# Three edits to a hybrid decoder layer on one core: condition and products moved at the start, output chunks fetched together, PE's feed-forward loop written out

## The reference, cut to what matters

```python
shift1, scale1, gate1, shift2, scale2, gate2 = adaln_terms(c, w_ada, b_ada)
h = rms_norm(x, g_pre_mix) * (1.0 + scale1) + shift1
z = einsum('btd,de->bte', h, w_in)
...
merged = (sigmoid(gm) * einsum('btw,wd->btd', hm, w_proj_m)
          + sigmoid(gd) * einsum('btw,wd->btd', hd, w_proj_d))
y = einsum('btd,de->bte', merged, w_out)
x = x + gate1 * rms_norm(y, g_post_mix)
h2 = rms_norm(x, g_pre_ffn) * (1.0 + scale2) + shift2
u = einsum('btd,df->btf', h2, w_up)           # a half: causal conv of width 3, then GELU
out = einsum('btf,fd->btd', gelu(conv(a)) * b, w_down)
x = x + gate2 * rms_norm(out, g_post_ffn)
```

## Time and profile before

| | us |
|---|---|
| three timed runs | 1811.71, 1811.73, 1812.12 |
| median | 1811.73 |
| the profiled execution, its own time | 1811.7 |
| its span in the profile | 1810.0 |
| PE busy in the span | 1749.2 (97%) |
| VectorE busy | 752.5 (42%) |
| ScalarE busy | 500.9 (28%) |
| GpSimd busy | 156.9 (9%) |

### The profile page before, as it was taken

How to read it: one execution, slowest core, us unless ns; L and a number is a source line. 1 busy time by engine, 2 the same in 40 slices (tenths; PEclk the granted TensorE clock), 3 DMA queues, 4 the chain that set the end, 5 groups by cost and what they waited for, 6 DMA issues and landing times. The chain is left out here.

```text
span 1810.0 us, 27372 instructions
## 1 busy us (share of the span) xinstructions
PE 1749.2 (97%) x11470; PEld 1655.8 (91%) x11470; DVE 752.5 (42%) x1017; ACT 500.9 (28%) x810; POOL 156.9 (9%) x231
## 2 busy tenths in 40 slices
PE   5999999999999999999999999999999999999998
PEld 5899888888888989999978899999999999999997
DVE  5522144544431146564543344424434434344245
ACT  4311134434343334431233331111211211211212
POOL 4010000000010014400023300000000000000001
PEclk8999999999999999999999999999999999999999
DMA  9665342232227577443432211111111021011104
GB/s 324 224 201 180 111 132 78 99 110 87 87 66 250 170 208 184 113 116 125 168 131 85 74 50 47 47 48 47 47 48 47 24 71 47 24 56 48 38 25 172
DMA packets 159707, 190.41 MB, mean 105 GB/s; under 512 B 13694, under 2 KB 138126, under 8 KB 159565
## 3 DMA queue, kind: packets, MB, share of 16 engines
q1 hardware_dynamic: 139368, 170.95, 29.5%
q10 hardware_dynamic: 19208, 17.43, 3.0%
q0 software_dynamic: 1008, 0.23, 0.1%
HBM read 146.70 MB, written 41.87 MB: 104 GB/s over the span
## 5 line engine op out<-in xcount | busy, mean ns | idle before, releaser
L158 PE MATMUL ps<-mg_hi,w_hi 128*128 128x352 f32 x1008 | 218.5, 325 | 6.0 <-issue 2.9
L158 PE MATMUL ps<-mg_hi,w_lo 128*128 128x352 f32 x1008 | 217.3, 323 | 0.0
L158 PE MATMUL ps<-mg_lo,w_hi 128*128 128x352 f32 x1008 | 217.0, 323 | 0.0
L158 PEld LDWEIGHTS ps<-mg_hi,w_hi 128*128 128x128 f32 x1008 | 171.4, 189 | 7.7 <-issue 5.6
L158 PEld LDWEIGHTS ps<-mg_hi,w_lo 128*128 128x128 f32 x1008 | 173.0, 188 | 0.0
L158 PEld LDWEIGHTS ps<-mg_lo,w_hi 128*128 128x128 f32 x1008 | 171.2, 188 | 0.0
L2808 DVE TENSOR_TENSOR f_t<-f_t,ps 128x1056 f32<-128x1056 f32 x80 | 100.3, 1253 | 151.2 <-PE ps L158 151.2
L143 DVE TENSOR_TENSOR w_lo<-w_raw,w_hi 128x2048 fp32r<-128x2048 f32 x61 | 141.3, 2316 | 51.6 <-ACT w_hi L139 51.6
L139 ACT ACTIVATE w_hi<-w_raw 128x2048 fp32r<-128x2048 f32 x61 | 116.7, 1914 | 121.1 <-PE ps L158 120.0
L1221 PE MATMUL ps<-acts_hi,w_hi 128*128 128x352 f32 x384 | 133.5, 348 | 8.1 <-ACT out_z L1074 3.8
L1337 PE MATMUL ps<-acts_hi,w_hi 128*128 128x352 f32 x384 | 128.6, 335 | 4.9 <-PEq L994 1.6
(11 more groups left out here) (412 smaller groups left out, 3066.8 us busy)
## 6 DMA issues: line engine op xcount, KB each, us to landing
w_raw<-in_w_in SPq DMA_DIRECT2D x22, 1024.0 KB, 5.8
w_raw<-in_w_up SPq DMA_DIRECT2D x22, 1024.0 KB, 5.1
w_ada_chunks<-in_w_ada ACTq DMA_DIRECT2D x16, 1024.0 KB, 7.6
w_raw<-in_w_down SPq DMA_DIRECT2D x11, 1024.0 KB, 4.9
z_scratch<-out_z SPq DMA_DIRECT2D x48, 176.0 KB, 1.8
z_scratch<-gate_ev SPq DMA_DIRECT2D x48, 176.0 KB, 3.7
w_ada_chunks<-in_w_ada SPq DMA_DIRECT2D x8, 1024.0 KB, 10.5
chunks<-z_scratch SPq DMA_DIRECT2D x24, 256.0 KB, 4.2
```

Source lines behind the costliest of these rows:

```text
L158: mm = pe.matmul(ps[:, bank + b, 0:TB], w[wi][:, k, j * P:(j + 1) * P], (a_hi, a_lo)[ai][:, k, b * TB:(b + 1) * TB], start=(n == 0), stop= ...
```

## The change

Three places are edited.

1. **The start.** `condition(0)` moves up: on PE from behind `x_tr(7)` to behind `x_tr(4)`, on ScalarE from behind `x_cols(7)` to behind `x_cols(5)`, and its transposes and columns likewise (VectorE makes the columns inside the loop over x tiles). On ScalarE the first chunk's high part is written in two pieces, blocks 0 and 1 (`W_FIRST`, 512 of 2048 elements) and the rest, and `condition(1)` stands between the two `acts_hi`. VectorE's low part has the same two pieces, the rest behind pair 1. PE's products of block 0 are reordered: high*high of both tiles first, which needs only the high parts of block 0, then `condition_tr(1)`, then low weights, then low activations.
2. **The output projection.** w_out chunks 2 and 3 get raw buffers of their own in the space of `acts_lo`, and are loaded one behind the other once the last tile that reads `acts_lo` is done (TILE5). The loads of the two x tiles follow at once.
3. **The feed-forward loop on PE alone** becomes a loop of the program that builds the kernel, so that its five iterations stand in the instruction stream one after another. The other engines keep their loops.

```diff
+        W_FIRST, W_REST = slice(0, 2 * NC_), slice(2 * NC_, CW)
...
-                    if t == NTT:
+                    if t == 7:
                         condition(0)
-                split_hi(act, 0, 16)
+                act.wait_ge(w_loaded[0], 16)
+                act.activation(w_hi[:, 0, W_FIRST], w_raw[:, 0, W_FIRST], ACT.Copy).then_inc(w_hi_first, 1)
                 for q in range(4):
-                    if q:
+                    if q > 1:
                         condition(q)
                     for i in range(2):
                         act.wait_ge(s_hm, 4 * q + 3 + i)
                         act.activation(acts_hi[:, 2 * q + i, :], x_t[:, 2 * q + i, :], ACT.Copy).then_inc(s_ahi, 1)
+                        if (q, i) == (0, 0):
+                            condition(1)
+                    if q == 0:
+                        act.activation(w_hi[:, 0, W_REST], w_raw[:, 0, W_REST], ACT.Copy).then_inc(w_hi_ready, 1)
...
+                for t in range(NTT + 2):
...
+                    if t == 8:
+                        dve.wait_ge(s_vect, 6)
+                        condition_cols(0)
...
-                    if q == 0:
-                        split_lo(dve, 0, 1)
+                    for part, hi_done, lo_done in ([(W_FIRST, w_hi_first, w_lo_first)], [(W_REST, w_hi_ready, w_lo_ready)], [], [])[q]:
+                        dve.wait_ge(hi_done, 1)
+                        dve.tensor_tensor(w_lo[:, 0, part], w_raw[:, 0, part], w_hi[:, 0, part].bitcast(F32), ALU.subtract).then_inc(lo_done, 1)
...
-                for t in range(3, 8):
-                    x_tr(t)
+                x_tr(3)
+                x_tr(4)
                 pe.wait_ge(s_vect, 6)
                 pe.wait_ge(s_sel, 3)
                 condition(0)
+                x_tr(5)
+                x_tr(6)
+                condition_tr(0)
+                x_tr(7)
                 x_tr(8)
-                condition_tr(0)
                 for half in range(2):
                     pe.wait_ge(s_xe[half], NTT)
                 condition(1)
-                pe.wait_ge(w_lo_ready, 1)
-                first_tiles(0)
+                pe.wait_ge(w_hi_first, 1)
+                pe.wait_ge(s_ahi, 1)
+                for j in range(2):
+                    first_products(0, 0, j)
                 condition_tr(1)
+                pe.wait_ge(w_lo_first, 1)
+                for j in range(2):
+                    first_products(0, 2, j)
+                pe.wait_ge(s_alo, 1)
+                for j in range(2):
+                    first_products(0, 1, j)
                 first_tiles(1)
                 condition(2)
+                pe.wait_ge(w_lo_ready, 1)
                 first_tiles(2)
...
+    xw_raw = [nc.alloc_sbuf_tensor_at(f"w_out_raw{i}", [P, CW], F32, offset=acts_lo_at + 4 * D_MODEL * (1, YS + 2)[i]) for i in range(2)]
...
+                sp.wait_ge(tile_done, TILE5)
                 for c in range(2, OUT_CHUNKS):
-                    load_chunk(sp, c % 2, w_cols(I["w_out"][0], c * NC_), KT, OUT0 + c - 1)
+                    sp.dma_start(xw_raw[c - 2][:].rearrange("p (k n) -> p k n", k=KT), w_cols(I["w_out"][0], c * NC_)).then_inc(w_loaded[c % 2], 16)
...
-                sp.wait_ge(tile_done, TILE5)
                 x_load(0)
...
-                    with pe.Fori(0, 2 * (NPAIR // 2) - 1, 2) as m:
+                    for m in range(0, 2 * (NPAIR // 2) - 1, 2):
```

More of the change, by code:

```diff
@@ L659, in condition_cols @@
                         ins_.then_inc(s_adat, 1)
+                for t in range(NTT + 2):
+                    if t < NTT:
+                        x_stat(t)
+                    if 1 <= t <= NTT:
+                        x_scale(t - 1)
+                    if t >= 2:
+                        x_cols(t - 2)
+                    if t == 4:
+                        tables()
+                    if t == 8:
+                        dve.wait_ge(s_vect, 6)
+                        condition_cols(0)
+                    if t == 0:
+                        dve.wait_ge(s_sel, 2)
+                        dve.tensor_reduce(sel[:], sel4[:].rearrange("p j t -> p t j"), AX_X, ALU.add).then_inc(s_sel, 1)
                 def slot(s):
@@ L669, in _ @@
                 for q in range(4):
-                    condition_cols(q)
+                    if q:
+                        condition_cols(q)
                     for half in range(2):
@@ L843, in slot, with first_products @@
                         condition_tr(pair_in(s - 1))
+                def first_products(k, n, j):
+                    w = [x[:, 0, :].rearrange("p (k n) -> p k n", k=KT) for x in (w_hi, w_lo)]
+                    wi, ai = ((0, 0), (0, 1), (1, 0))[n]
+                    for b in range(NTB):
+                        mm = pe.matmul(ps[:, 3 * j + b, 0:TB], w[wi][:, k, j * P:(j + 1) * P],
+                                       (acts_hi, acts_lo)[ai][:, k, b * TB:(b + 1) * TB],
+                                       start=(k == 0 and n == 0), stop=(k == KT - 1 and n == 2))
+                    return mm
                 def first_tiles(k):
                     pe.wait_ge(s_alo, k + 1)
[L848 removed]
                     for j in range(2):
[L850 to L854 removed]
+                        for n in range(3):
+                            mm = first_products(k, n, j)
                         if k == KT - 1:
```

25 lines of the change are left out of this document (4 added, 21 removed).

## The result

The changed kernel takes 1801.86 us (median of 5 runs, 1800.76 to 1803.91) against 1811.73 of before, a ratio of 0.9947 with a 95% interval of 0.9935 to 0.9960: 9.6 us less, between 7.2 and 11.8. Forecast were 1800.6, within 1798.8 to 1805.2. The profiled execution took 1801.9 (span 1800.1), the one of before 1811.7 (span 1810.0), so 9.9 us have to be found between the two traces.

A forecast was written before the change was run, and what follows sets the result against it. PE, busy nearly throughout, was taken as the bound, so only its idle or half-clock time could be won. Terms of -4.4, -1.7 and -5.0 sum to -11.1 from 1811.7, giving 1800.6 us, range 1798.8 to 1805.2.

The forecast's parts named there:

- the start: Start: earlier first products and full clock end the first tiles near 66.4 instead of 71.4; -5.0 us.
- The prediction is wrong if the clock falls near 33: Start: sign against the forecast, which had PE's granted clock stay full until the first tiles' end.
- Output projection: Output projection: PE's 1.63 us wait for the low part of w_out chunk 3 goes; -1.7 us, bounds 0 and -1.8.
- Feed-forward loop: Feed-forward part: four pieces between PE's iterations go when the loop is written out; -4.4 us, bounds 4.0 to 4.7.
- the overlap: Feed-forward loop: matmul rows overlap successors by about 0.16 us, hidden by a gap, so each piece may cost 0.16 more.
- the other engines' late steps: Feed-forward loop: rival that another engine's late step makes the pieces, so they stay; -6.7 us, 1805.0, chance 0.06.
- the slow rival: Feed-forward loop: rival that straight code starves PE, being fetched whole and ahead of use; 1834 us, chance 0.02.
- the jump itself: Feed-forward loop: the pieces of 0.92 to 1.18 us come from PE's loop jump, which breaks instruction prefetch.
- The nine packets of an iteration: Feed-forward loop: nine instruction packets already land in one iteration with no gap inside, so straight code is fetched as now.
- the one on the clock: Start: PE is not idle longer than 1.1 us from 25 to the first tiles' end, so the clock stays full.
- The rival that I gave 0.15: Start: clock falls from about 33 for 6.5 us, losing 3.3; start gives 1.7, time 1803.9, chance 0.15.
- Moving the condition up wins almost nothing by itself: Start: the last x tile's square then stands behind the condition, so line 680 starts at 33.7 instead of 33.86.

The follow-up runs named there:

- experiment 2: Kernel before with only the start's split weight and new product order, condition pair 0 at its old place; ratio 0.9983 to the kernel before.
- experiment 5: Kernel before with only PE's feed-forward loop written out; ratio 0.9978 to the kernel before.
- experiment 7: Kernel after, with PE's feed-forward iterations 1 to 3 in a loop and 4 and 5 written out; ratio 0.9956 to the kernel before.
- experiment 8: Kernel before with the feed-forward loops of SyncE, GpSimd, ScalarE and VectorE written out, PE's kept; ratio 1.0000 to the kernel before.
- experiment 11: Kernel before with 29 filler matmuls in PE's wait ahead of the first products, PE's loop kept; ratio 0.9982 to the kernel before.
- experiment 12: Kernel before with 20 filler matmuls in PE's wait ahead of the first products, PE's loop kept; 1808.2 us, ratio 0.9983 to the kernel before.
- experiment 4: Kernel after with nine filler matmuls in three of PE's gaps at the start; 1799.32 us, ratio 0.9933 to the kernel before.
- experiment 1: Kernel before with all the start edits and nothing else; ratio 0.9985 to the kernel before.
- experiment 3: Kernel before with only condition pair 0 moved up, weights split whole and products in old order; ratio 0.9994 to the kernel before.
- experiment 9: Kernel after with nine fillers, and the last x tile's square moved earlier on ScalarE; ratio 0.9940 to the kernel before.
- experiment 6: Kernel before with only the output projection's edit; ratio 0.9991 to the kernel before.

## Why the prediction was right, and where it was not

The time was right: 1801.9 for a forecast of 1800.6. In part that was luck, since the start gave 2.1 us less than forecast and the other two terms 1.1 more. By its own sign, "The prediction is wrong if the clock falls near 33", its account of the start failed: the clock fell at 31.7.

**Output projection, -1.7 forecast, -2.1 measured,** of which 1.63 is the wait that is gone. The steps came as reckoned: chunk 3 landed 7.8 us after the end of the last tile (899.2 - 891.45; forecast 8.0), its low part was done 12.0 us after it (12.2), and PE passed with 1.0 us of slack (1.2). The x tiles queued behind the chunk did not take enough of its bandwidth to matter. Over all profiles the stretch is shorter by 1.5 to 2.3 us (experiment 2's left out), and the forecast 1.7 lies within that.

**Feed-forward loop, -4.4 forecast, -5.06 measured,** outside the bounds of 4.0 to 4.7. The mis-sized term is the overlap. The pieces sum to 4.06 us. I added 0.16 for each as its upper end; it was (5.06 - 4.06) / 4 = 0.25. The pieces themselves differ between executions: in the other kernels that keep the four jumps the matmuls took 714.2 to 715.3 us, 3.9 to 5.0 more than 710.25. So 4.4 lies within what the term can be, and the trace of before was at its upper end. The readings around it held: the pieces stand at PE's jump alone (experiments 5, 7, 8), the other engines' late steps are not their cause, and no wait for the fetch of the straight code shows. It needs fewer packets than the loop (90 against 99), so the slow rival had no ground.

One step behind the right number was still too short. I took the jump itself for the cause. It costs only if the body is fetched again: with the loop at another address (experiments 11 and 12) PE jumps four times and loses nothing. The counts fit. PE's program of before is 16,339 instructions of 64 bytes, 63.8 packets of 16.4 KB; with its body of 1759 instructions fetched four times more, at nine packets each, that makes 100, one more than the 99 counted. With the fillers, 64 packets are the program once. The nine packets of an iteration, which I used to say that straight code costs no more than the loop, were the trace of the fault itself.

The Trainium skill bears on this in "Runtime: NRT & Kernel Launch", Instruction fetch mechanics: PE's instruction memory is given as 128 KiB, filled in blocks of 16 KiB, and a taken branch is said to wait for a fetch when its target is not in the current window. It speaks of a window of two blocks; experiments 11 and 12 speak against that for PE, since there a body of 112.6 KB, which 128 KiB could hold, was looped over with no packet in an iteration and no wait. Before, each jump did wait for a fetch, 0.92 to 1.18 us by the chain, as the rule has it. The 108 ns that "Advanced Engine Details and Errata" states for a compare-and-branch was seen in neither: 1.0 to 1.3 us where the body is fetched, nothing visible where it is not.

**The start, -5.0 forecast, -2.9 measured.** The step that failed is the one on the clock: "PE is not idle for longer than 1.1 us between 25 and the first tiles' end, so I let it stay at full clock". It was not idle for longer than 0.85, nor for longer than 0.77 before the fall, and the clock fell at 31.7 all the same. Yet gaps of this size do not explain the fall alone: the kernel before had 0.61 and 0.85 us between x tiles 5, 6 and 7, with nothing but transposes between, and its clock stayed at 1.00 from 24 to 36 (its rows, of PE, behind x tile 5):

```profile
25.66 1.09 PE L800 MATMUL ps<-ident,x_in 128*128 128x128 f32 x8 [0.61 <-DVE x_in L603]
27.60 1.09 PE L800 MATMUL ps<-ident,x_in 128*128 128x128 f32 x8 [0.85 <-DVE x_in L603]
```

The rival that I gave 0.15 was what happened, in a milder form: it had the tiles at 1.7 us gained, and 2.9 came. The clock was low for 6.8 us, as long as that rival had it (6.5), but not all of it was work that others waited for: PE was busy for 4.72 of the 6 us from 32 to 38. With the gaps filled (experiment 4) the start gives 71.4 - 66.1 = 5.3 against the same trace of before, and its moments meet the forecast: 33.7, 35.76, 39.63 and 66.1 for 33.7, 35.7, 39.6 and 66.4. The difference between the two kernels is 2.4 us at the tiles, of which the clock cost about 1.8 and a later landing of the condition's weights 0.6; in experiments 1 and 7, which have the same start and no such delay, the clock cost 2.0 to 2.3.

Of the 2.2 us by which the products were late (37.91 against 35.7), about 1.0 lies ahead of the scaling of the blocks (34.73 against 33.69 in experiment 4) and 1.1 behind it (3.18 us from there to the products against 2.07; the second condition pair at half rate). Of the 1.0, some 0.6 is the landing of the condition's second chunk, at 25.68 against 25.02; the rest is x tiles at half rate.

**"Moving the condition up wins almost nothing by itself"** held: tile 7 was scaled late, at 30.02, 0.07 us behind the statistics that wait for the last square, and experiment 3 gives nothing that a measurement can tell, within its 2.7 us. Experiment 2 shows the other side. Whether the square's place is what the move lacks stays open, since experiment 9 was spoiled by its own fillers.

**The sum** came out within 1.3 us because misses cancelled: the loop gave 0.7 and the output projection 0.4 more, and the start 2.1 less than forecast.

## What stays open

Why the body stays with PE in experiments 11 and 12 and not in the kernel before is not settled. Shown is that it was fetched again with the loop at its old address or a few instructions beside it (experiments 1 to 3, 6 to 8), and not with it 80 or 116 instructions further. My rule of touched packets explains 116 and not 80. Its start may be counted from a wrong zero, but it allows 34 starting places in a row (7 x 256 - 1759 + 1), and the two kernels' loops start 36 instructions apart. That the fillers do it by something else than the address is not excluded; that they would do so a thousand microseconds later by anything but the address seems unlikely, and it was only argued. A row of kernels with 10 to 200 idle instructions put at another place would settle both.

Why the clock fell at 31.7 is open as well. Idle time alone does not explain it, as said above. Nor does it that the work was mostly transposes: before, the clock rose at 23 behind transposes alone. The same fillers in PE's transpose mode would tell whether it is the idle time or the kind of work that counts.

## What to carry to other kernels

Look at the instruction queue of an engine that loops for long. If packets land in every iteration, the body is being fetched again and each jump may cost about a microsecond; writing the loop out removes that, and so may a shift of its address, which also means that an unrelated edit ahead of a loop may win or lose the same amount.

A forecast for a stretch in which PE transposes and waits by turns has to carry both clocks: with gaps of 0.6 to 0.9 us it stayed full in one trace here and fell in others. Such gaps can be filled with matmuls that nobody reads. Fit their length to the gap, measured at full rate: too many cost what they save.

Where single runs scatter by several microseconds, read a small edit at its own place in the trace, against the next fixed event on the chain, and use the medians only to see that it arrives. Look first at how that place scatters in traces of kernels that share its code: here one stretch was steady within 0.02 us and another spread over 3.9.

## What the runs showed of the hardware that was not expected

- Loop jumps of PE with a body of 112.6 KB: 1.0 to 1.3 us each (714.2 to 715.3 us against 710.2 for the matmuls with four jumps) when nine packets of 16.4 KB were fetched in every iteration, nothing visible when none was, in the same code at an address 116 or 80 instructions further on.
- The granted clock fell at 31.7 us with PE idle for no more than 0.77 us at a time since 26 us (0.30 and 0.77) and little but transposes for work. With products of the identity as fillers it was at 1.00 in all windows there (experiment 4).
- The clock column can say 1.00 where the rates say half: in experiment 2, condition pair 0 took 2.84 us instead of 1.93 in windows shown at 1.00. Until the clock's first fall in a trace, the time of a known group is the safer sign. The earlier trace rows lie behind a fall, and the rates agree with them: 3.67 us for 16 transposes until 23, 1.10 for 8 behind it.
